# A product of zeros behind each tile in the second half of the decay scans, and a gate moved ahead of stream 13

## What is computed

```
qk  = (q_t . k_s) * exp(a_ts - m_t)      for s <= t (or s >= t, backward)
h_t = sum_s qk_ts v_s / max(|sum_s qk_ts|, exp(-m_t))
h   = h_forward + h_backward ; normed over the head, gated
```

```
y_t = sum_s (C_t . B_s) * exp(cs_t - cs_s) * dt_s * x_s      (both directions, summed)
y   = (y + x * d_skip) * silu(z) ; RMS-normed over groups of 128 columns
```

## Time and profile before

| | us |
|---|---|
| median of 3 runs | 2123.17 (2122.65 to 2130.05) |
| the profiled execution, its own time | 2123.46 |
| its span, first to last instruction | 2121.3 |
| mean granted clock of TensorE, share of full speed | 0.893 |
| PE busy | 1743.2 (82%) |
| DVE busy | 1164.8 (55%) |
| ACT busy | 878.9 (41%) |
| POOL busy | 662.5 (31%) |

### The profile page before, as it was taken

The page is one execution under the profiler, slowest core; times in us unless marked ns, Lnnn a source line. Parts: engine busy times, 40 slices in busy tenths (PEclk is TensorE's granted clock), DMA queues, the critical chain, the costliest instruction groups (busy, mean ns, idle before and its releaser), DMA issues. The chain is left out here.

```text
span 2121.3 us, 22435 instructions
## 1 busy us (share of the span) xinstructions
PE 1743.2 (82%) x7978; PEld 1347.0 (63%) x7978; DVE 1164.8 (55%) x1693; ACT 878.9 (41%) x1294; POOL 662.5 (31%) x348
## 2 busy tenths in 40 slices
PE   5999995859991799997666995499697689999997
PEld 4876532647870686742555884388367477888885
DVE  3926565649975564645556995592466414143241
ACT  2246555127872235655314884322645322111111
POOL 2337523101110333731401120144352023444441
PEclk8999987859995999997767997799889899999998
DMA  4201111057963311020117994320000122222221
GB/s 174 80 32 40 40 40 59 1 223 299 371 252 150 117 70 42 1 66 14 60 40 291 359 380 180 120 100 23 17 3 1 60 99 100 99 94 87 96 79 49
DMA packets 40476, 233.83 MB, mean 110 GB/s; under 512 B 9316, under 2 KB 9700, under 8 KB 20660
## 3 DMA queue, kind: packets, MB, share of 16 engines
q1 hardware_dynamic: 31012, 215.42, 26.9%
q0 software_dynamic: 9216, 16.80, 2.2%
q10 hardware_dynamic: 144, 0.26, 0.0%
HBM read 226.00 MB, written 23.23 MB: 117 GB/s over the span
## 5 line engine op out<-in xcount | busy, mean ns | idle before, releaser
L256 PE MATMUL bank<-XS,WS 128*128 128x512 f32 x864 | 201.9, 396 | 22.3 <-DVE WS L381 20.8
L2213 POOL TENSOR_TENSOR WS<-ring,WS 128x2048 fp32r<-128x2048 f32 x31 | 149.5, 4822 | 190.7 <-ACT WS L2205 190.7
L256 PEld LDWEIGHTS bank<-XS,WS 128*128 128x128 f32 x864 | 165.4, 192 | 58.4 <-DVE WS L381 21.3
L1235 PE MATMUL bank<-WS,XS 128*128 128x512 f32 x768 | 187.3, 400 | 1.1 <-DVE XS L1355 1.1
L2234 PE MATMUL bank<-XS,WS 128*128 128x512 f32 x768 | 174.9, 389 | 3.0 <-DVEq L2263 3.0
L2252 PE MATMUL bank<-WS,US 128*128 128x512 f32 x768 | 174.7, 389 | 0.0
L2205 ACT CAST WS<-ring 128x2048 fp32r<-128x2048 f32 x31 | 59.2, 1911 | 271.7 <-PE bank L2234 144.1
L1235 PEld LDWEIGHTS bank<-WS,XS 128*128 128x128 f32 x768 | 145.2, 193 | 31.3 <-DVE XS L1355 1.9
L2234 PEld LDWEIGHTS bank<-XS,WS 128*128 128x128 f32 x768 | 144.1, 188 | 33.1 <-DVEq L2263 3.2
L2252 PEld LDWEIGHTS bank<-WS,US 128*128 128x128 f32 x768 | 144.1, 188 | 29.9
L1572 PE MATMUL bank<-XS,WS 128*128 128x512 f32 (+1 forms) x600 | 136.4, 389 | 2.7 <-POOLq L1623 2.7
(11 more groups left out here) (487 smaller groups left out, 3534.8 us busy)
## 6 DMA issues: line engine op xcount, KB each, us to landing
raw<-in_w_exp SPq DMA_DIRECT2D x16, 2048.0 KB, 13.4
DN<-in_w_exp SPq DMA_DIRECT2D x32, 1024.0 KB
ring<-in_w_ff SPq DMA_DIRECT2D x32, 1024.0 KB, 4.7
raw<-in_w_in SPq DMA_DIRECT2D x20, 1024.0 KB, 4.8
GU<-in_w_exp SPq DMA_DIRECT2D x8, 2048.0 KB, 15.7
XT<-in_w_exp SPq DMA_DIRECT2D x8, 2048.0 KB, 16.1
ring<-in_w_in SPq DMA_DIRECT2D x12, 1024.0 KB, 4.8
raw<-in_w_out SPq DMA_DIRECT2D x8, 1024.0 KB, 5.0
```

The costliest lines, as they stand in the source:

```text
L256: last = pe.matmul(m.ps[g % 8][:, :], WS[:, i % 2, hw, at:at + P], XS[:, hx, k, :], start=(step == 0), stop=(step == 3 * KD - 1))
L1235: last = pe.matmul(m.ps[2 + e % 2][:, :], r.XS[:, e % 2, hx, 4 * half + k, :], r.WS[:, half, hw, k * S:(k + 1) * S], start=(half == 0 and ...
L2213: pool.tensor_tensor(f.WS[:, q % 2, 1, :], f.ring[:, q % 4, :], f.WS[:, q % 2, 0, :].bitcast(F32), ALU.subtract).then_inc(w_low, 1)
```

## The change

A new helper on PE, `idle_product`, multiplies the identity with 256 columns of zeros into the first 256 columns of a bank. It is issued behind each tile of streams 8 to 11 (behind the `base` product in stream 11), into bank 7, and behind each tile of streams 13 and 14 and tiles 0 to 2 of stream 15, into bank 6: 27 a pass, 54 in an execution. Stream 12 has none. In streams 8 to 11 nothing of value is in bank 7, since stream 12 starts it anew; in streams 13 to 15 bank 6 has been read by `y_gate(0)`, for which PE waits once, behind tile 13.0. `y_gate(0)` moves on DVE from behind W of 13.2 to behind W of 12.3.

```diff
+            def idle_product(bank):
+                pe.matmul(bank[:, 0:256], m.ident[:, :], m.zeros[:, 0:256], start=True, stop=True, skip_group_check=True)
+
...
                     last.then_inc(applied, 1)
                     if s == last_of_base[b] and b < 5:
                         base(b + 1, j)
+                    if 8 <= s <= 11:
+                        idle_product(m.ps[7])
+                    elif s >= 13 and (s, j) != (15, 3):
+                        if (s, j) == (13, 0):
+                            pe.wait_ge(y_gated, 1)
+                        idle_product(m.ps[6])
             y_sum(1)
...
                     if j == 1 and 1 <= s <= 8:
                         denominators(s - 1)
+                    if (s, j) == (12, 3):
+                        y_gate(0)
                     if j == 2:
                         if s == 8:
                             inverse_denominators()
...
                         elif s == 12:
                             centre()
-                        elif s == 13:
-                            y_gate(0)
                         elif s == 15:
```

## The result

The changed kernel takes 2149.34 us (median of 4 runs, 2148.63 to 2150.28), the kernel before 2123.81 (4 runs): ratio 1.0114, interval 1.0094 to 1.0135. Slower, as forecast, but by 25.5 us where 14 were forecast, and outside the range (2125 to 2146). Run again on another occasion it took 2148.47 beside 2127.75: 1.0084, 1.0053 to 1.0116. Against the kernel before, whose 27 runs beside the first experiments spread from 2116 to 2133 with a median of 2125.55, the loss is some 21 to 26 us. The profiled execution took 2150.28 us, its span is 2148.1.

The account below looks back on a forecast made before the run. TensorE was taken as the bound in most of the stage's second half. Per pass, 13.15 us of cost less 9.45 of clock is 3.7, plus 0.85, 1.7 and 0.85: 7.1; two passes: 2123.2 + 14.2 = 2137, range 2125 to 2146.

Parts of the forecast that it names:

- The bound: Second half of the scans stage: TensorE is the bound from 297.83 to 323.31 and from 330.51 to 336.52.
- The price of a product: On TensorE's path: 0.79 us between narrow tiles, 0.43 beside a wide product, 1.35 between narrow tiles at 1.2 GHz.
- The lost pair of tiles: Tiles 9.3 and 10.0 ran side by side; the product between them costs 0.85 us more at 2.4 GHz.
- The gate: y_gate(0), 2.1 us on VectorE, moved ahead of W of 13.0; about 0.2 us a pass shows.
- The free products: Eight a pass, after 8.0, 8.1, 8.2, 13.3, 14.3 and 15.0 to 15.2, forecast to cost nothing.
- The clock: Full clock could return 9.45 us a pass; remaining low clock was charged 0.85, 1.7 and 0.85 us.
- stretch 1: TensorE from 297.83 to 310.83, 13.0 us; 7.4 at 2.4 GHz, so up to 5.6 us could be had.
- stretch 2: TensorE from 330.51 to 336.52, all at 1.2 GHz; 3.0 of its 6.0 us could be had.
- rival 1: The clock stays high throughout: 3.7 us longer per pass, 2131 us in all; chance 0.20.
- Outside the stage: Stages the change doesn't touch: the forecast sum gave them no term.
- The signs set ahead: Variance products 5 to 7.5 us later, ScalarE's wait behind them under 4, first y sum ending 6 to 8 later.

Follow-up runs that it names:

- the first experiments: Follow-up kernels compared with the kernel before on the same chip, beginning with the gate move alone: 2126.64 us against 2125.55.
- real data: The changed kernel with all 27 products a pass taken from the convolved inputs instead of identity and zeros: 2147.67 us, ratio 1.0095.
- the last kernel: Against the kernel before: gate at its old place, 16 products of zeros a pass, mostly 512 columns, only in TensorE's pauses: 2107.95 us, ratio 0.9924.

## Why the prediction was wrong

- *The bound.* Right: no pause from 298.27 to 333.08, and every product there moved what follows it.
- *The price of a product.* Right between narrow tiles at 2.4 GHz: from 309.50 a tile of 512 columns takes 1.00 us with its way out, and a product 0.63 (308.87 to 309.50), together 0.78 over the tile's own 0.85, forecast 0.79. Right at 1.2 GHz as well: 1.15 for the product (298.89 to 300.04) and 0.19 more for the tile behind it, 1.34 for 1.35. Ahead of a wide product 0.43 was too little: 0.63 at 305.33, 0.54 at 332.54, some 0.6 us a pass. Streams 10.3 to 12.0 came out at 11.39, forecast 11.4.
- *The lost pair of tiles.* Right, 1.63 us from start to start.
- *The gate.* Forecast 0.2 behind the products; the stretch it is in came out at 6.02, forecast 5.8. Of the 0.2 over, half is the dearer product ahead of the variance and half the gate: the first columns of 13.0 come 0.3 us later than those of stream 12 end. Alone, without the product after 11.3 as cover, it costs 1.05.
- *The free products.* Right in time on TensorE; wrong in that they carry the count of instructions over the point at which the pause in the feed-forward stage appears.
- *The clock: the step that failed.* I gave the low clock of stretch 1 a half chance of 3.4 us and that of stretch 2 3.4 us, 0.85 and 1.7 us. It fell in both stretches in all the changed kernel's passes, and in stretch 1 in all ten passes with this kernel's streams 8 to 11. In stretch 1 it was low for 6.8, 3.4, 6.8 and 6.8 us in four passes, a cost of half of that, 3.4 or 1.7 instead of 0.85; in stretch 2 6.8, 6.8, 3.4, 3.4. With the dearer wide neighbours that makes 11.1 and 9.3 us for 7.1. The advice of the Trainium skill ("TensorE: Matmul & The Clock Gate", the table of goals in "Why this matters for your kernels") to keep idle gaps short, by which rival 1 has no fall at all, would have given less still; here the trace does not agree, as a wait shortened to 2.56 us did not spare the clock. Stretch 2 was no case for it: its wait, forecast 3.4 us and measured 3.58, is longer than the 2.94 us after which the clock fell in the kernel before.
- *Outside the stage: the term I left out.* I took it for zero, and it came out at 6.4 us. The pause of 2.1 us and the low clock behind it (at most 1.7 us) are in both traces of the changed kernel, up to 3.8 of the 6.4 us; but without the pause the kernel was no faster (2148.71), and with it the part behind the second pass was as short as before in one trace (1107.2, real data). Two traces of the kernel before differ by 3.4 us in this part. How much of the 6.4 us comes from the change stays open.
- *The signs set ahead.* Met: the wait behind the variance products is under 4 us (3.58), 9.3 and 10.0 no longer start together, a product between narrow tiles costs its 0.79. Missed, mostly by the clock: the variance products came 9.3 and 7.8 us later after 8.0 (5 to 7.5 forecast), the first y sum ended 11.1 and 9.3 later (6 to 8), and the low clock of stretch 1 was 6.8 us in the first pass, not at most 3.4.

The forecast's mechanism and sign hold. Its size missed, in the traces, by 12.6 us: 6.2 in the stage (4.0 and 2.2 in the two passes), most of it the clock term, and 6.4 outside it. In the ratio the miss depends on the occasion as well, since the kernel before measured 2123 to 2128.

## What to carry to other kernels

Work added to keep TensorE's clock up pays only in the places where TensorE waits; behind each tile of a bound stretch it costs its columns and the changes of form, more than the clock gives back (here 13 us a pass by the working ahead, of which the traces bear out the prices, against at most 9.45). Fill each pause up to just before its end, and the gain that the clock promises comes (here 17 us of 18.9 in the medians); few wide products do it with fewer instructions. A length of low clock taken from one trace is a draw: look at a second trace of the same kernel before giving it a number.

## What was not expected of the hardware

- The low clock after the same 4.73 us wait lasted 13.6 us in seven passes with the kernel before's streams 8 to 11 and 3.4 us in the eighth. In that one it fell 6.7 us after tile 8.0, just ahead of 8.3, in the others 4.5 to 4.8 us after it.
- Adding 27 small products (108 matrix and weight-load records a pass) brings a pause of 1.6 to 2.2 us without a wait in a stage some 0.9 ms later; with 23 it is absent. The queue of instructions shows 60 packets in the kernel before and 70 with 27 products as with 23, so the packets alone don't tell; that a late fetch of code causes it was argued and not shown.
- Two products with 64 stationary columns in different halves run side by side, with starts 0.01 us apart (two tiles of 512 columns that both start at 302.85 in the last kernel), also when one of them is a product of zeros that belongs to nothing.
